# Modulation products of a two-layer diffusion kernel: from multiply-adds on VectorE to plain fp32 matmuls in four 32-column tiles on TensorE

## What the kernel computes

```
mx = split(silu(c) @ mod_w[l] + mod_b[l], 9)          # for the latent tokens
mh = split(silu(c_ctx) @ mod_w[l] + mod_b[l], 9)      # for the context tokens
x = x + 0.5 * mx[2] * swiglu(modulate(rms_norm(x, norm_ffn1[l]), mx[0], mx[1]), w_in, w_out)
h = h + 0.5 * mh[2] * swiglu(modulate(rms_norm(h, norm_ffn1[l]), mh[0], mh[1]), w_in, w_out)
yx, yh = token_mixer(modulate(rms_norm(x), mx[3], mx[4]), modulate(rms_norm(h), mh[3], mh[4]), ...)
x, h = x + mx[5] * yx, h + mh[5] * yh
...                                                   # second FFN with mx[6..8], mh[6..8]
# modulate(u, shift, scale) = u * (1 + scale) + shift
# swiglu(u) = (silu(g) * a) @ w_out,  [a, g] = u @ w_in,  w_in 1024 x 5632, w_out 2816 x 1024
```

## Time and profile before

| | before |
|---|---|
| time, median of 3 runs | 2201.52 us (2200.64 to 2205.01) |
| span of the profiled execution, first to last instruction | 2205.8 us |
| TensorE matmul busy | 2081.2 us |
| TensorE weight load busy | 1686.1 us |
| VectorE busy | 1412.4 us |
| ScalarE busy | 651.9 us |
| GpSimd busy | 1017.0 us |
| mean granted TensorE clock | 0.974 |

### The profile page before, as it was taken

How to read it: one execution, slowest core, us unless ns; L and a number is a source line. 1 busy time by engine, 2 the same in 40 slices (tenths; PEclk the granted TensorE clock), 3 DMA queues, 4 the chain that set the end, 5 groups by cost and what they waited for, 6 DMA issues and landing times.

```text
span 2205.8 us, 29876 instructions
## 1 busy us (share of the span) xinstructions
PE 2081.2 (94%) x10122; PEld 1686.1 (76%) x10122; DVE 1412.4 (64%) x1940; ACT 651.9 (30%) x1019; POOL 1017.0 (46%) x423
## 2 busy tenths in 40 slices
PE   6898899999999999999999999999999889999998
PEld 2677777887657888777877787778778666999998
DVE  7998999657374123698289649936983846665213
ACT  3211121243342223511221242122224334444343
POOL 2353355444201444454455445544544420875886
PEclk9999999999999999999999999999999999998999
DMA  8453565244201333454355234534534330654564
GB/s 279 159 172 117 185 195 161 66 103 106 64 1 29 95 95 95 122 171 137 104 157 169 71 108 152 174 112 143 152 110 110 101 88 1 181 155 131 172 189 125
DMA packets 445424, 278.95 MB, mean 126 GB/s; under 512 B 33906, under 2 KB 407148, under 8 KB 445356
## 3 DMA queue, kind: packets, MB, share of 16 engines
q1 hardware_dynamic: 401868, 206.79, 33.1%
q10 hardware_dynamic: 43360, 71.05, 9.8%
q0 software_dynamic: 128, 0.23, 0.0%
HBM read 276.98 MB, written 1.05 MB: 126 GB/s over the span
## 4 chain that ended last, share of the span: by engine, by line
PE 51%; DVE 22%; issue 20%; POOL 4%; ACT 2%; DVEq 1%; DMA 0%; ACTq 0%; POOLq 0%; SPq 0%
PE bank L1128 15%; PE bank L1130 15%; PE bank L1129 15%; DVE acc L814 4%; POOL w_lo L391 4%; DVE h_hi L867 3%; DVE h_lo L869 3%; DVE u_lo L789 2%; PE bank L1394 1%; PE bank L1342 1%; DVE hf L861 1%; DVE tmp L774 1%; DVE mtmp L829 1%; PE bank L1378 1%; DVE acc_hi L821 1%
## 5 line engine op out<-in xcount | busy, mean ns | idle before, releaser
L391 POOL TENSOR_TENSOR w_lo<-w_raw,w_hi 128x1024 fp32r<-128x1024 f32 (+2 forms) x412 | 1014.1, 2479 | 1176.0 <-ACT w_hi L423 1176.0
L1128 PE MATMUL bank<-u_hi,w_hi 128*128 128x512 f32 (+1 forms) x2016 | 746.7, 370 | 22.5 <-DVE u_lo L789 20.5
L1129 PE MATMUL bank<-u_lo,w_hi 128*128 128x512 f32 (+1 forms) x2016 | 731.8, 363 | 0.0
L1130 PE MATMUL bank<-u_hi,w_lo 128*128 128x512 f32 (+1 forms) x2016 | 731.2, 363 | 0.0
L1128 PEld LDWEIGHTS bank<-u_hi,w_hi 128*128 128x128 f32 x2016 | 390.5, 194 | 86.6 <-DVE u_lo L789 19.8
L423 ACT ACTIVATE w_hi<-w_raw 128x1024 fp32r<-128x1024 f32 (+2 forms) x412 | 384.8, 968 | 203.3 <-PE bank L1130 161.8
L1129 PEld LDWEIGHTS bank<-u_lo,w_hi 128*128 128x128 f32 x2016 | 390.3, 194 | 55.9 <-issue 1.3
L1130 PEld LDWEIGHTS bank<-u_hi,w_lo 128*128 128x128 f32 x2016 | 389.1, 193 | 57.3
L814 DVE SCALAR_TENSOR_TENSOR acc<-mod_w,sil,acc 128x512 f32<-128x512 f32 x448 | 315.3, 778 | 0.0
L1130 PE MATMUL bank<-h_hi,w_lo 128*128 128x512 f32 (+1 forms) x704 | 260.4, 370 | 0.0
L1128 PE MATMUL bank<-h_hi,w_hi 128*128 128x512 f32 (+1 forms) x704 | 258.3, 367 | 1.8 <-DVE x L845 1.5
(11 more groups left out here) (159 smaller groups left out, 1875.0 us busy)
## 6 DMA issues: line engine op xcount, KB each, us to landing
w_raw<-in_ffn_w_in SPq DMA_DIRECT2D x176, 512.0 KB, 3.9
mod_w<-in_mod_w ACTq DMA_DIRECT2D x64, 1024.0 KB, 6.4
w_raw<-in_w_in SPq DMA_DIRECT2D x68, 512.0 KB, 3.8
w_raw<-in_ffn_w_out SPq DMA_DIRECT2D x64, 384.0 KB, 3.4
w_raw<-in_ffn_w_out SPq DMA_DIRECT2D x64, 320.0 KB, 3.4
mod_first<-in_mod_w SPq DMA_DIRECT2D x4, 2048.0 KB, 19.7
w_raw<-in_w_o SPq DMA_DIRECT2D x16, 512.0 KB, 4.0
w_raw<-in_w_in SPq DMA_DIRECT2D x16, 256.0 KB, 4.2
```

The costliest lines, as they stand in the source:

```text
L391: pool.tensor_tensor(w_lo[:, slot, 0:n, :], w_raw[:, slot, 0:n, :], w_hi[:, slot, 0:n, :].bitcast(F32), ALU.subtract).then_inc(S("w_lo_rea ...
L1128: pe.matmul(dst, w_hi[:, slot, kk, :], hi_[:, ka, 0:n], start=start, stop=False)
L1129: pe.matmul(dst, w_hi[:, slot, kk, :], lo_[:, ka, 0:n], start=False, stop=False)
L1130: return pe.matmul(dst, w_lo[:, slot, kk, :], hi_[:, ka, 0:n], start=False, stop=stop)
```

## The change

The 16 multiply-adds, the split, the sum with ones and the masked reduction are replaced. `sil` becomes 32 columns wide for each chunk of 128 rows (two silu columns and 30 of zeros). `mod_rounds` does the 8 chunks of a group as 8 plain fp32 matmuls of 512 columns: chunk j of each half goes to the 32 partitions from 32j of bank 6, so that four neighbouring matmuls have four different column tiles, and the second half adds to the first. ScalarE copies bank 6 to `mod_part` (`copy_mod`), TensorE turns it in four 128x128 blocks into bank 7 (`mod_turn`), and VectorE sums the four tiles' columns in one reduction of 32 elements (`mod_extract`). In a loop body the rounds stand behind the first chunk and the turn behind the second.

The four groups of the start go the same way, in the order 0, 2, 1, 3. Two are done in front of the first norm, two after TensorE has used the norm's first four channel chunks; VectorE waits for these before it scales the fifth. On SP's queue the first two weight blocks move ahead of the third and fourth group of `mod_first`.

```diff
-    BG_BASE = {k: 1 + sum(BG_COUNT[o] for o in BG if o < k) for k in BG}
+    BG_BASE = {k: N_START + sum(BG_COUNT[o] for o in BG if o < k) for k in BG}
+    START_GROUPS = (0, 2, 1, 3)
...
-    sil = sb("sil", [P, 2, DC])
+    sil = sb("sil", [P, DC, 32])
+    mod_part = sb("mod_part", [P, MG])
...
+        for G in range(2):
+            load_first(G)
+        for j in range(2):
+            load(phases[order[0]], [(0, P, 0, DC, t["ffn1_w_in"][0].rearrange("(k p) c -> p k c", p=P)[:, :, j * D_FF:j * D_FF + P])], j, 0, 0, 2)
+        for G in range(2, N_START):
+            load_first(G)
...
                 if k == 0 and d == DC // 2:
-                    copy_mod_rows(N_START - 1)
+                    for G in range(2, N_START):
+                        copy_mod(G)
                     load_mod(BG_BASE[0, 1], *mod_plan(0, 1, BG_BASE[0, 1]))
...
+        def copy_mod(G):
+
+            act.wait_ge(S("mod_mm"), 2 * G + 2)
+            wait(act, S("mod_turned"), G)
+            act.activation(mod_part[:], bank[:, 6, :], ACT.Copy).then_inc(S("mod_copied"), 1)
...
-                        if c == 1 and mods and more and not (start and k):
-                            G = mods[0] + i + 1 - (1 if half == 0 and k else 0)
-                            load_mod(G, *mod_plan(l, f, G))
+                        if c == 1 and mods and not (start and k):
+                            G = mods[0] + i - (1 if half == 0 and k else 0)
+                            copy_mod(G)
+                            if more:
+                                load_mod(G + 1, *mod_plan(l, f, G + 1))
...
         root_of(0)
+        for G in range(2):
+            copy_mod(G)
         first_hi(order[0])
...
-        def mod_products(G, first=False):
...
-        def mod_split(G, first=False):
...
+        def mod_extract(G, layer, group):
+
+            dve.wait_ge(S("mod_turned"), G + 1)
+            parts = bank[:, 7, :].rearrange("p (a j r) -> p r a j", a=MGC, j=4)[:, 0:2]
+            dve.tensor_reduce(modcol[:, layer, :, bass.ds(group * MGC, MGC)], parts, AX_X, ALU.add).then_inc(S("mod_kept"), 1)
...
+        def start_columns(h):
+
+            for G in range(2 * h, 2 * h + 2):
+                mod_extract(G, 0, START_GROUPS[G])
+            dve.wait_ge(S("mod_kept"), 2 * h + 2)
+            columns_norm(0, DC // 2 * h, DC // 2 * h + DC // 2)
         rstd_of(0)
+        start_columns(0)
...
-                if first and k == 0 and kk == 1:
-                    turn_mod(N_START - 1, N_START)
+                if first and k == 0 and kk == DC // 2 - 1:
+                    for G in range(2, N_START):
+                        mod_rounds(G)
+                        mod_turn(G)
...
-        def mod_reduce(G, first=False):
...
+        def mod_rounds(G):
+
+            wait(pe, S("mod_copied"), G)
+            for kh in range(2):
...
+                for j in range(MK):
+                    last = pe.matmul(bank[32 * j:32 * j + 32, 6, :], sil[:, MK * kh + j, :], w[:, j, :], start=kh == 0, stop=kh == 1)
+                last.then_inc(S("mod_mm"), 1)
+
+        def mod_turn(G):
+
+            pe.wait_ge(S("mod_copied"), G + 1)
+            wait(pe, S("mod_kept"), G)
+            for a in range(MGC):
+                last = pe.transpose(bank[:, 7, P * a:P * a + P], mod_part[:, P * a:P * a + P], ident[:])
+            last.then_inc(S("mod_turned"), 1)
...
                     for c in range(2):
                         hidden(c + i * 2, c, i)
-                    if mods and not (half == 0 and k and isinstance(i, int)):
-                        mod_reduce(mods[0] + i - (1 if half == 0 and k else 0))
+                        if with_mods:
+                            (mod_rounds, mod_turn)[c](G)
...
         pe.wait_ge(S("sil_ready"), 1)
-        mod_group(1)
         mean_square(0)
-        mod_group(2)
-        mod_reduce(0, first=True)
-        mod_group(3, 0, 2)
-        turn_mod(1, 3)
-        mod_group(3, 2, DC)
+        for G in range(2):
+            mod_rounds(G)
+            mod_turn(G)
```

More of the change, by code:

```diff
@@ L294, in mods_done @@
     def mods_done(l, f):
-        return 1 + sum(BG_COUNT[k] for k in BG if k <= (l, f))
+        return N_START + sum(BG_COUNT[k] for k in BG if k <= (l, f))
     block = ctx.enter_context(nc.Block())
@@ L1170, in mean_square @@
             pe.matmul(bank[:, 4, 0:n], ones_mean[:], ssq[:, 0:n], start=True, stop=True).then_inc(S("ms_ready"), 1)
-        def mod_reduce(G, first=False):
-            _, acc_hi, acc_lo, _ = sums_start if first else sums_bg
-            pe.wait_ge(S("acc_ready"), G + 1)
+        def mod_rounds(G):
+            wait(pe, S("mod_copied"), G)
+            for kh in range(2):
+                if isinstance(G, int) and G < N_START:
+                    pe.wait_ge(first_loaded[G], 16)
+                    w = mod_first[:, START_GROUPS[G], MK * kh:MK * kh + MK, :]
+                else:
+                    pe.wait_ge(mod_loaded[kh], (G - N_START + 1) * 16)
+                    w = mod_w[:, kh]
+                for j in range(MK):
[3 more added lines that the diff above has]
+            pe.wait_ge(S("mod_copied"), G + 1)
             wait(pe, S("mod_kept"), G)
-            for v in range(2):
-                pe.matmul(bank[:, 6 + v, :], ones_r[:], acc_hi[:, v, :], start=True, stop=False)
-                last = pe.matmul(bank[:, 6 + v, :], ones_r[:], acc_lo[:, v, :], start=False, stop=True)
-            last.then_inc(S("red_ready"), 1)
+            for a in range(MGC):
+                last = pe.transpose(bank[:, 7, P * a:P * a + P], mod_part[:, P * a:P * a + P], ident[:])
+            last.then_inc(S("mod_turned"), 1)
         def ffn(l, f):
@@ L1198, in body @@
                 def body(i):
+                    with_mods = mods and not (half == 0 and k and isinstance(i, int))
+                    G = mods[0] + i - (1 if half == 0 and k else 0) if with_mods else None
                     for c in range(2):
                         hidden(c + i * 2, c, i)
-                    if mods and not (half == 0 and k and isinstance(i, int)):
-                        mod_reduce(mods[0] + i - (1 if half == 0 and k else 0))
+                        if with_mods:
+                            (mod_rounds, mod_turn)[c](G)
                 turns(pe, FH // 2, body, peel=half == 0)
@@ L1239, in turn_x @@
             last.then_inc(S("x_turned"), 1)
-        def mod_group(g, k0=0, k1=DC):
-            pe.wait_ge(first_loaded[g], 16)
-            for kk in range(k0, k1):
-                last = pe.matmul(bank[0:2, g, :], sil[:, :, kk], mod_first[:, g, kk, :], start=kk == 0, stop=kk == DC - 1)
-            if k1 == DC:
-                last.then_inc(S("rows_mm"), 1)
-        def turn_mod(g0, g1):
-            pe.wait_ge(S("mod_rows_ready"), g1 - 1)
-            for g in range(g0, g1):
-                for a in range(MGC):
-                    o = 2 * (MGC * g + a)
-                    last = pe.transpose(bank[:, 5, o:o + 2], mod_rows[:, g, P * a:P * a + P], ident[0:2, 0:2])
-            last.then_inc(S("modt_ready"), 1)
         pe.wait_ge(S("vec_ready"), 1)
```

93 lines of the change are left out of this document (20 added, 73 removed).

## The result

The changed kernel takes 2186.86 us (median of 4 runs, 2182.64 to 2189.76), beside 2202.57 us for the kernel before, measured with it (4 runs, 2200.64 to 2205.01). The ratio is 0.9918, interval 0.99 to 0.9937: faster by 0.8%, 15.7 us. On a second chip six more runs gave 2183.30 us beside 2208.87 us, a ratio of 0.9888 (0.9869 to 0.9907) and 25.6 us, so the size of the gain is known only as 16 to 26 us. The forecast was 2253 us and slower, and the direction was wrong. The time lies inside the stated range, but near rival A's 2180 us and far from the middle value.

A forecast was written before the change was run, and what follows sets the result against it. TensorE, busy 94%, was taken as nearly the bound, waiting for VectorE's modulation work. New TensorE work 150 less 106.4 gave +44 us, the start +7: 2201.5 + 51, about 2253 us, range 2172 to 2287.

The forecast's parts named there:

- rival A: Rounds on four column tiles at once: 1.71 us a round, 2.6 a group, time about 2180 us; chance 0.32.
- middle value: Rounds on TensorE with passes overlapping by pairs: 3.84 us, between 1.71 and 6.83; time about 2253 us, chance 0.44.
- (a): The rounds, 8 calls a group on TensorE: taken as 3.84 us, with ends of 1.71 and 6.83.
- The 106.4 us: Cost of the 32 background groups before the change, 3.3 us each, all of it expected to go.
- The turn with the changes: Per group on TensorE: four transposes, 0.5 us, and four changes between kinds of matmul, 0.4 us.
- The deciding point of A: Rounds under 2.4 us put a group below 3.3 us, so that the changed kernel is faster.
- the turn waiting for ScalarE: Named way to be wrong: ScalarE's copy not hidden ahead of the turn, 0.6 us a group, 19 us.
- other waits covered by those that went: Named way to be wrong: the waits that go were covering others of like length in the same bodies.
- the one place that gains: The "out" stretch, forecast at 91 us in place of 95.1.
- The start: Work up to the end of the first pair: about 73.5 us in place of 66.6, a cost of +7 us.
- the product at 59.46: TensorE product in the start before the change, taken as the fifth channel chunk's, 7.1 us before the pair's end.
- VectorE's load: VectorE busy for some nine tenths or more of stretches with groups; about 500 us to go, leaving about 915.

The follow-up runs named there:

- tile-by-tile run: The changed kernel with a tile's two products next to each other, in place of all four tiles' first calls and then their second; 2187.52 us.
- one-tile run: The changed kernel with all eight products of a group on the first column tile, in place of four tiles; 2361.49 us.

## Why the prediction was wrong

**The step that failed** is in (a): "if matmuls start in order only the second pass of one call can overlap the first pass of the next". It made a round 9 x 0.427 = 3.84 us; measured are 1.85. Rounds of 1.85 with the other terms as forecast make a group of 2.75, 32 of them 88, and -18 in the background, which is rival A. The tile-by-tile run refutes the premise and the one-tile run shows the other end. The middle value came from no row: the earlier trace rows had nothing of two tiles, and I took an order of starts as given where the ends, 1.71 and 6.83, were all that was known. The measured values are 1.85 and 6.98, each about 0.15 above its end. The group as a whole is 2.60 us, rival A's 2.6.

**Tiles on a page and here.** The Trainium skill, "TensorE: Matmul & The Clock Gate", Part 3, has matmuls on different tiles start some 4 ns apart and a gain of 2.38 for three tiles. Here four starts lie in one slice of 0.21 us and four tiles gain 3.8. Its other sentence, that matmuls stay in program order, was what I leaned on; of passes on different tiles the run of tile by tile shows otherwise.

**Right.** The 106.4 us, 3.3 us a group, as all that could be gained: the stretches after are TensorE's own work and nothing more, at clock 1.00. The turn with the changes was forecast at 0.9 us; the group's 2.6 us less four waves of 0.43 leave 0.9. Nothing waits for the copy in the bodies. The deciding point of A, rounds under 2.4 us, held. Two ways in which it could have been wrong, the turn waiting for ScalarE and other waits covered by those that went, did not come true.

**Half right.** The "out" part was named as the one place that gains, and it has more than half of the first FFN's gain (12.6 of 20.0 us in three stretches), because its four groups cost 5.6 us each before. The start cost 6.5 us with a forecast of 7, but by other parts. The first two groups were done 3.5 us earlier (34.5, not 38), and the two in the middle took 6.5 us (54.36 to 60.8) in place of 10.3. Against that, from the end of the first two to the first product it was 12.4 us in place of 6, because remainders of GpSimd stood beside VectorE's columns and scalings, and the two waits were followed by 3.6 and 5.7 us at the lower clock. That the sum came out near 7 is luck. The forecast followed ScalarE's rounding into its own queue only; it did not ask what GpSimd, which comes next in that chain, would run into, though half of that collision stands in the trace of the kernel before. It also called the product at 59.46 that of the fifth channel chunk. It is the fourth: that kernel's stop lies in front of the fourth chunk's `u_lo`, so its 7.1 us to the end of the pair hold five chunks, where four are left after the change. With short rounds rival A put the start at +2, which was too little by 4.5 us.

**VectorE's load** was taken rightly as what lengthens the stretches; the run that keeps such a load shows stretches of about the old length with no wait for the modulation sum.

**A slip in the range.** Its lower end, A with 0.4 us less a group, was given as 2172. From A's 2180 less 32 x 0.4 it is 2167. The measured time is above both.

## What to carry to other kernels

When an overlap is in no row, its two ends are what is known; a value between them needs a mechanism that a row shows, and if the two ends lie on different sides of the deciding point, that is where the chances belong. A wait that goes is worth what the engine behind it is relieved of: here the run that kept the load and dropped the wait gained nothing that could be measured (0.9989). When an engine's work is moved ahead of a norm, follow it to the engine that is fed by it, and keep GpSimd's wide instructions away from the short chain of small VectorE operations that TensorE waits for.

## What the runs showed of the hardware that was not expected

- Sixteen passes of plain fp32, 32 stationary columns and 512 moving, take 1.85 us on four column tiles and 6.98 us on one (clock 1.00). A pass that waits for its tile does not hold up passes for other tiles, as far as the tile-by-tile run (waves of four, 0.43 us apart) lets one infer. Eight weight loads of such calls go in within 0.16 us.
- Changing into column tiles and back costs 0.3 to 0.4 us in all (2.04 us for a single round, 1.65 to 1.74 for one behind another), in a stretch of 128-column fp32r matmuls.
- A VectorE operation on 4 or 8 columns, 0.16 us by itself, took 2.2 to 2.3 us beside a GpSimd remainder of 128x1024, four times in a row beside four of them. The kernel before has it too, twice.
- The first attention, in the same work, ran at a granted clock of 1.00 in the changed kernel's profile and of 0.62 in the tile-by-tile run's, over 12 us, and took 4.1 us longer there.
